# The weight panels' split moves from GpSimd to ScalarE and VectorE, in four slots

## What is computed

```
first block, per layer:
  x = x + 0.5 * swiglu(rmsnorm(x), w_ffn1_in, w_ffn1_out)          # D_FF = 2816
  h = rmsnorm(x);  proj = h @ w_in
  y_ret = (silu(rg) * rmsnorm(retention(rope(rq), rope(rk), rv))) @ w_o_ret    # 4 heads of 128
  y_fox = forgetting_attention(fq, fk, fv, log_sigmoid(ff + b)) @ w_o_fox      # 8 heads of 64
  x = x + (sigmoid(gate_r) * y_ret + sigmoid(gate_f) * y_fox) @ w_out
  x = x + 0.5 * swiglu(rmsnorm(x), w_ffn2_in, w_ffn2_out)
x = rmsnorm(x)
second block, per layer:
  h = rmsnorm(x) @ w_in_2, split into the inputs of four branches and a gate
  y = [window attention with sinks, gated convolution, latent attention, stick-breaking attention]
  x = x + rmsnorm((rmsnorm_per_group(y) * silu(gate)) @ w_out_2)
```

## Time and profile before

| | us |
|---|---|
| median of three runs | 3171.14 |
| the runs | 3172.47, 3171.14, 3154.9 |
| profiled execution, first to last instruction | 3161.7 |
| PE busy | 3000.1 (95%) |
| DVE busy | 1414.9 (45%) |
| ACT busy | 680.9 (22%) |
| POOL busy | 2047.7 (65%) |

### The profile page before, as it was taken

The page is one execution under the profiler, slowest core; times in us unless marked ns, Lnnn a source line. Parts: engine busy times, 40 slices in busy tenths (PEclk is TensorE's granted clock), DMA queues, the critical chain, the costliest instruction groups (busy, mean ns, idle before and its releaser), DMA issues.

```text
span 3161.7 us, 38115 instructions
## 1 busy us (share of the span) xinstructions
PE 3000.1 (95%) x13442; PEld 2394.4 (76%) x13442; DVE 1414.9 (45%) x1627; ACT 680.9 (22%) x1190; POOL 2047.7 (65%) x925
## 2 busy tenths in 40 slices
PE   7999988999999999999998899999998999989996
PEld 5888876778788887888877677778886877777775
DVE  6442234544744405443054534654415444554445
ACT  2221002122122201221002122222200223422253
POOL 5777765636777777877775535777776643365324
PEclk9999999999999999999999999999999999999998
DMA  3222222112222222222221211222222211122111
GB/s 127 93 93 93 93 100 71 66 47 74 93 88 97 93 93 81 94 96 95 93 104 67 71 49 60 93 93 93 93 93 86 74 54 42 46 75 73 47 34 54
DMA packets 69361, 251.59 MB, mean 80 GB/s; under 512 B 7696, under 2 KB 7824, under 8 KB 69008
## 3 DMA queue, kind: packets, MB, share of 16 engines
q1 hardware_dynamic: 68400, 246.46, 22.9%
q10 hardware_dynamic: 864, 3.79, 0.3%
HBM read 248.13 MB, written 2.10 MB: 79 GB/s over the span
## 4 chain that ended last, share of the span: by engine, by line
PE 82%; DVE 12%; issue 4%; ACT 1%; DVEq 0%; DMA 0%; ACTq 0%; SPq 0%
PE bank L459 22%; PE bank L460 22%; PE bank L461 22%; DVE xh L1377 2%; DVE ssq L1397 2%; PE bank L559 1%; PE bank L614 1%; PE bank L802 1%; PE bank L561 1%; PE bank L560 1%; PE bank L624 1%; PE bank L591 1%; PE bank L680 1%; DVE qr L1477 1%; PE bank L732 1%
## 5 line engine op out<-in xcount | busy, mean ns | idle before, releaser
L438 POOL TENSOR_TENSOR wh<-raw,one 128x1024 fp32r<-128x1024 f32 x460 | 885.2, 1924 | 1048.0 <-PE bank L461 964.3
L442 POOL TENSOR_TENSOR wl<-raw,wh 128x1024 fp32r<-128x1024 f32 x460 | 1162.3, 2527 | 36.1
L459 PE MATMUL bank<-xh,wh 128*128 128x512 f32 x2384 | 960.5, 403 | 23.9 <-DVE start_d L1945 10.5
L460 PE MATMUL bank<-xl,wh 128*128 128x512 f32 x2384 | 948.0, 398 | 0.0
L461 PE MATMUL bank<-xh,wl 128*128 128x512 f32 x2384 | 947.3, 397 | 0.0
L459 PEld LDWEIGHTS bank<-xh,wh 128*128 128x128 f32 x2384 | 452.3, 190 | 139.9 <-DVE xl L1379 23.3
L461 PEld LDWEIGHTS bank<-xh,wl 128*128 128x128 f32 x2384 | 451.5, 189 | 109.5
L460 PEld LDWEIGHTS bank<-xl,wh 128*128 128x128 f32 x2384 | 452.3, 190 | 106.3 <-issue 1.9
L460 PE MATMUL bank<-ul,wh 128*128 (+1 forms) x704 | 280.9, 399 | 0.0
L459 PE MATMUL bank<-uh,wh 128*128 (+1 forms) x704 | 277.4, 394 | 0.0
L461 PE MATMUL bank<-uh,wl 128*128 (+1 forms) x704 | 276.0, 392 | 0.0
(11 more groups left out here) (356 smaller groups left out, 3369.2 us busy)
## 6 DMA issues: line engine op xcount, KB each, us to landing
raw<-stream SPq DMA_DIRECT2D x460, 512.0 KB, 3.3
x<-x_t SPq DMA_DIRECT2D x4, 512.0 KB, 8.6
dec<-decay ACTq DMA_DIRECT2D x2, 1024.0 KB, 5.2
out<-x SPq DMA_DIRECT2D x8, 256.0 KB, 2.0
rp<-rope ACTq DMA_DIRECT2D x2, 512.0 KB, 6.4
cst<-const SPq DMA_DIRECT2D x1, 708.5 KB, 10.6
ffraw<-ff_w ACTq DMA_DIRECT2D x2, 316.0 KB, 7.4
posi<-pos SPq DMA_DIRECT2D x1, 256.0 KB, 11.2
```

Of the source, the lines that this page charges most:

```text
L438: pool.tensor_tensor(wh[:, slot, :], raw[:, n, :], one[:].to_broadcast([P, PANEL]), ALU.mult)\
L442: pool.tensor_tensor(wl[:, slot, :], raw[:, n, :], wh[:, slot, :].bitcast(F32), ALU.subtract).then_inc(split_lo, 1)
L459: pe.matmul(o, wh[:, s, c], rhs_h, start=first, stop=False)
L460: pe.matmul(o, wh[:, s, c], rhs_l, start=False, stop=False)
```

## The change

POOL does nothing any more. A panel's `wh` is made by `high` on ACT, a copy that rounds, and its `wl` by `low` on DVE, a subtraction. Both are placed by hand between the other steps of these engines, for the panel `LEAD = 3` behind the one that PE has reached there. `wh` and `wl` have four slots each instead of two, `raw` two instead of four, and `wl` is allocated before `wh`. `At` is a position in the stream as fours plus a rest, so that slot numbers stay known inside loops. The loops over the hybrid layers, the `rg` heads, the squares and the middle pairs of `forgetting` are written out; `ffn_in` on ACT goes two pairs at a time and the inner loop of `ffn_out` four panels at a time.

```diff
-RAW_SLOTS, SPLIT_SLOTS = 4, 2
+RAW_SLOTS, SLOTS = 2, 4
+LEAD = 3
+class At:
+    def __add__(self, panels):
+        return At(self.four, self.more + panels)
+    def fours(self, count):
+        return At(self.four + count, self.more)
+    def slot(self):
+        return self.more % SLOTS
+    def done(self, panels=1):
+        return self.four * SLOTS + (self.more + panels)
+    def raw(self):
+        return self.more % RAW_SLOTS
...
-        @block.gpsimd
-        def _(pool):
-            def split(n, g, first=False):
-                slot = n % SPLIT_SLOTS
-                pool.wait_ge(raw_in[n], 16 * (g + 1))
-                if not (first and n < SPLIT_SLOTS):
-                    pool.wait_ge(panel_done, g * RAW_SLOTS + (n + 1 - SPLIT_SLOTS))
-                pool.tensor_tensor(wh[:, slot, :], raw[:, n, :], one[:].to_broadcast([P, PANEL]), ALU.mult)\
-                    .then_inc(split_hi, 1)
-                pool.wait_ge(split_hi, g * RAW_SLOTS + (n + 1))
-                pool.tensor_tensor(wl[:, slot, :], raw[:, n, :], wh[:, slot, :].bitcast(F32),
-                                   ALU.subtract).then_inc(split_lo, 1)
...
@@ ACT @@
+            def high(at, first=False):
+                act.wait_ge(raw_in[at.raw], at.landed())
+                if not first:
+                    act.wait_ge(panel_done, at.done(1 - SLOTS))
+                act.activation(wh[:, at.slot, :], raw[:, at.raw, :], ACT.Copy).then_inc(split_hi, 1)
...
@@ DVE @@
+            def low(at):
+                dve.wait_ge(split_hi, at.done())
+                dve.tensor_tensor(wl[:, at.slot, :], raw[:, at.raw, :], wh[:, at.slot, :].bitcast(F32),
+                                  ALU.subtract).then_inc(split_lo, 1)
...
@@ ffn_in on ACT @@
+                def pair(j, at, first):
+                    if not first:
+                        high(at + LEAD)
                     act.wait_ge(*fin.at(it, "A"))
                     act.activation(sa[:], ta[:], ACT.Silu).then_inc(fin_act.sem, 1)
+                    high(at + 1 + LEAD)
                     act.wait_ge(*fin.at(it, "U"))
                     act.activation(uh[:, j, :], u32[:], ACT.Copy).then_inc(fin_act.sem, 1)
...
@@ ffn_in on DVE @@
                     scaled(ta[:], a[:], fin)
+                    if not first:
+                        low(at + LEAD)
                     scaled(tb[:], b[:], fin)
                     dve.tensor_tensor(u32[:], sa[:], tb[:], ALU.mult).then_inc(fin.sem, 1)
+                    low(at + 1 + LEAD)
                     dve.tensor_tensor(ul[:, j, :], u32[:], uh[:, j, :].bitcast(F32), ALU.subtract)\
...
@@ ffn_out on DVE, behind the steps of residual tile d @@
                     add_squares(n, d)
+                    for p in rest_done(d):
+                        low(idx + KT_MAJOR + p + LEAD)
...
@@ hybrid on DVE, behind the rotations of the latent queries @@
+                ahead(BT_UQ)
                 for i in range(2):
                     dve.scalar_tensor_tensor(out=dq[:, i, :], in0=bank[i][:], scalar=BDH ** -0.5, in1=rstd[:],
                                              op0=ALU.mult, op1=ALU.mult).then_inc(pj.sem, 1)
+                    ahead(BT_DQ + i)
...
@@ hybrid on ACT, ahead of the Silus of the gates @@
+                ahead(BT_GATE + KD - 2, 2)
                 for d in range(KD):
                     act.wait_ge(*gate_in.at(m * KD + d, "G"))
                     act.activation(gates[:, d, :], gates[:, d, :], ACT.Silu).then_inc(gate_s.sem, 1)
...
@@ start on DVE @@
                 prepare(0, d, 0)
+                if d == 0:
+                    low(At(0, 0))
             for d in range(KD):
                 add_squares(0, d)
+                if d in (4, 7):
+                    low(At(0, d // 3))
+            low(At(0, LEAD))
```

More of the change, by code:

```diff
@@ L671, in forgetting @@
                 pair(0, True, False)
[L672 removed]
+                for t2 in range(1, pairs - 1):
                     pair(t2, False, False)
@@ L1040, in _ @@
             chain_bc(FINAL, 7)
-            with pe.Fori(0, DEPTH) as m:
+            for m in range(DEPTH):
                 hybrid(m)
@@ L1135, in pair @@
                         fox_probs(it + 1, 0)
+                high(idx + LEAD)
+                high(idx + 1 + LEAD)
                 fox_probs(l * pairs, 0)
                 pair(0, True, False)
-                with act.Fori(1, pairs - 1) as t2:
+                for t2 in range(1, pairs - 1):
                     pair(t2, False, False)
@@ L1191, in hybrid, with ahead @@
                 n = FINAL + 1 + m
+                q0 = At(0, SECOND + m * LAYER2)
+                def ahead(tile, tiles=1):
+                    for i in range(tile, tile + tiles):
+                        if q0.more + i + LEAD < N_PANELS:
+                            high(q0 + i + LEAD)
+                ahead(BT_TM + (m == 0), 3 + (m > 0))
                 chain_std(n, 0, hyb_sq.at(m, "U"))
                 for i in range(2):
+                    ahead(BT_CQ + i)
                     act.wait_ge(*pj.at(m, f"Q{i}"))
                     act.activation(qsq[:, i, :], cq[:, i, :], ACT.Square).then_inc(lat_act.sem, 1)
+                ahead(BT_CKV)
                 act.wait_ge(*pj.at(m, "KV"))
                 act.activation(ksq[:], ckv[:], ACT.Square).then_inc(lat_act.sem, 1)
+                ahead(BT_AK)
                 act.wait_ge(*lat_pe.at(m, "COL"))
@@ L1321, in _ @@
             act.activation(start_a[:], eps[:], ACT.Copy).then_inc(rg_act.sem, 1)
-            squares(0)
+            high(At(0, 0), True)
+            squares(0, lambda d: d in (3, 7) and high(At(0, d // 4 + 1), True))
+            high(At(0, LEAD), True)
             act.wait_ge(const_in, 16)
@@ L1338, in _ @@
                 act.dma_start(ffraw[:], ff_w[l]).then_inc(tab_in, 16)
+                high(p0 + AT_RV + LEAD)
                 chain_std(l * 3 + 1, 0)
-                with act.Fori(0, RH) as h:
+                for p in range(1, KD):
+                    high(p0 + AT_RV + p + LEAD)
+                for h in range(RH):
+                    high(p0 + AT_RG + h + LEAD)
                     act.wait_ge(*rg.at(l * RH + h, "T"))
@@ L1366, in _ @@
             operands(0)
-            with act.Fori(0, DEPTH) as m:
+            for m in range(DEPTH):
                 hybrid(m)
@@ L1438, in ffn_in @@
                     for q in range(2):
-                        pair(i * 2 + q, bank[2 * q], bank[2 * q + 1], idx + i * 4 + 2 * q)
+                        pair(i * 2 + q, bank[2 * q], bank[2 * q + 1], (idx + 2 * q).fours(i))
             def ffn_out(f, n, idx):
+                with dve.Fori(0, KT_MAJOR // SLOTS) as i:
+                    for q in range(SLOTS):
+                        low((idx + q + LEAD).fours(i))
                 rest = KF - KT_MAJOR
@@ L1691, in hybrid, with ahead @@
             def hybrid(m):
-                q0 = SECOND + m * LAYER2
+                q0 = At(0, SECOND + m * LAYER2)
                 n = FINAL + 1 + m
-                norm_chain(n, 1)
-                dve.wait_ge(panel_done, q0 + BT_TM + KD // 2)
+                def ahead(tile, tiles=1):
+                    for i in range(tile, tile + tiles):
+                        if q0.more + i + LEAD < N_PANELS:
+                            low(q0 + i + LEAD)
+                ahead(BT_TM + (m == 0), 2 + (m > 0))
+                norm_chain(n, 1, lambda: ahead(BT_TM + 3))
+                dve.wait_ge(panel_done, (q0 + BT_TM).done(KD // 2))
                 for t in range(TT):
@@ L2020, in _ @@
                     operand_lo(0, d - 1)
-            with dve.Fori(0, DEPTH) as m:
+            for m in range(DEPTH):
                 hybrid(m)
```

357 lines of the change are left out of this document (209 added, 148 removed).

## The result

| | kernel before | changed kernel |
|---|---|---|
| median (lowest to highest), us | 3166.4 (3154.9 to 3172.5), 4 runs | 3045.9 (3044.0 to 3048.0), 4 runs |
| ratio of the runs, 95% interval | | 0.9619 [0.9591, 0.9648] |
| span of the profiled execution | 3161.7 | 3044.6 (its time 3046.4) |

The change is worth 120 us by the medians and 117.1 us between the two profiled spans.

What follows compares the result with a forecast made beforehand. TensorE was taken as the bound, busy 3000.1 of 3161.7 us, its waits due to GpSimd slowing DVE. Stage gains less give-backs sum to 84.4 us: from a median of 3171 to 3087, range 3062 to 3126 (8 of 10).

Steps and rivals of the forecast that it cites:

- The cause: DVE steps on two SBUF tiles wait out GpSimd's step in progress; the same add takes 0.69 or 2.77 us.
- the costs of the new steps: Per panel, ACT's copy `wh` takes 1.06 us and DVE's subtraction `wl` 1.23 us.
- the steady state at no cost: Within the feed-forward the new split keeps up with PE, with about 9 us of slack; cost nothing.
- the seams of the feed-forward: Gains: ends into the mixer 20.7 us, into the second block 6.4, start of layer 2 6.2.
- the wait at the third latent panel: Hybrid layers, ahead of `dq`: PE idles about 2.0 us for a `wl` in place of 6.8.
- No rival: Alternatives: late seams 3125 (0.22); GpSimd not the cause 3196 (0.03); raw-slot loop 3225 (0.03); more gain 3067 (0.10).
- the fourth's 3067: No PE wait in the gating or before panel 1, clock up all through: 20 us less; chance 0.10.
- matmuls at 0.233 us: Matmul pace stays at 0.233 us; another pace would prove the prediction wrong.
- head 0 of the retention: Decay chain shrinks 5.4 us, two `low` add 2.5: 2.9 gained, 3.8 of the 6.64 wait and low clock stay.
- The start: Kernel start: 2.5 us gained, despite a first `low` delaying PE 1.2 and a wait of some 5 for panel 1.
- `dq`: Both hybrid layers: PE's 6.78 us waits for rotations shrink by 4.8 each, 9.5 us together.
- The hybrid layers' rest: Shorter `spl` steps gain 7.5 us and the gating gives back 2.6 in both layers: 4.9.

Runs made afterwards that it cites:

- e1: Changed kernel with an unused 128x1 tensor where the removed `one` stood, so tiles behind it start 32 bytes further on; 3056.6 us.
- e9: Changed kernel with the `low` inside each rotation moved behind the product with the swapped halves; 3051.2 us.
- e2: Kernel before, with `uh`, merged heads and head outputs shifted to 0 modulo 256 and ACT's loop over the retention-gate Silus written out; 3146.6 us.
- e14: Kernel before, GpSimd's split untouched, with all big TensorE operands at the same place modulo 256 (distance 0); 3143.4 us.
- e10: Changed kernel with a second 128x1024 subtraction, read by nobody, behind each `low` on DVE but the first four; 3089.9 us.
- e3: Changed kernel with unused 128-byte tensors ahead of `x` and `raw`, so `xh` and `xl` start at 0 modulo 256 instead of 128; 3024.4 us.
- e12: Changed kernel with `wl` and `wh` 192 bytes further on, at 128 modulo 256 instead of 192, all else in place; 3022.5 us.
- e7: Changed kernel with `xh`, `xl`, `ygh` and `ygl` at 0 modulo 256 and panel 1's split made earlier at the start; 3020.8 us.
- e5: Changed kernel with `wl` back on GpSimd as its subtraction, `wh` staying on ACT and no `low` on DVE; 3077.4 us.

## Why the prediction was right in kind and short by 33 us

**What held.** The cause (a DVE step of two SBUF tiles waits GpSimd's step out), the costs of the new steps (1.06 and 1.23 forecast, 1.05 and 1.22 measured), the steady state at no cost, and the seams of the feed-forward: 20.7 forecast and 21.3 measured, 6.4 and 6.7, 6.2 and 5.1. GpSimd is empty, `ssq` is not waited for at the mixer, the wait at the third latent panel is there. No rival came true: the time lies below even the fourth's 3067, but PE still waits for panel 1 (4.2 us) and in the gating (2.0).

**The failed step: "matmuls at 0.233 us" for all of them.** The text named another pace as what would prove it wrong, and so it was: 2880 matmuls at 0.2289 instead of 0.2333 us, 12.7 us by count, 10.7 in e1. The forecast had put this term at nothing. The diff shows that tiles move (`one` goes, slots change), and the trace of before shows two paces at clock 1.00, 0.233 in `ffn_in` and 0.230 in the token-major stage. I read both and took the difference to be one of the kind of matmul.

**The step mis-sized most: head 0 of the retention**, "five steps of two SBUF tiles shrink by the mean 1.09", "and two `low` add 2.5: 2.9 gained, some 3.8 of 6.64 stay". It gained 6.7 of wait and 2.1 of clock in each layer, 8.8 for 2.9. DVE before, then after:

```profile
493.50 1.94 DVE L1986 SCALAR_TENSOR_TENSOR fq<-fq 72x512 f32<-72x512 f32 x1 [6.58 <-ACT fq L1348]
495.48 3.30 DVE L1989 TENSOR_TENSOR_SCAN cum<-cst,fq 72x512 f32<-72x512 f32 x1
...
501.74 1.86 DVE L1475 TENSOR_TENSOR diag<-tq,rp 128x512 f32<-128x512 f32 x1
```
```profile
471.20 0.69 DVE L2114 SCALAR_TENSOR_TENSOR fq<-fq 72x512 f32<-72x512 f32 x1 [4.08 <-ACT fq L1431]
471.92 1.22 DVE L2117 TENSOR_TENSOR_SCAN cum<-cst,fq 72x512 f32<-72x512 f32 x1
...
476.10 0.69 DVE L1567 TENSOR_TENSOR diag<-tq,rp 128x512 f32<-128x512 f32 x1
476.71 1.22 DVE L1454 TENSOR_TENSOR wl<-raw,wh 128x1024 fp32r<-128x1024 f32 x1
```

Three errors, all one way. The mean was taken where single rows stood: the scan alone shrank by 2.08, the five steps by 7.6. The `low` was priced in full at 1.23, and cost some 0.4 (e9). And the chain began 1.4 us earlier, counted at the same place of PE's work, because a table load of 1.28 us on ACT ahead of it went. Of ACT's 153 table loads 104 went: in the loops before, each round loaded its table anew (88 loads in `ffn_in`, 8 for the retention gates), and with the rounds, or the first ones of a loop, written out 4 and 2 are left. The chain adds up to the 6.7: 1.4 of start, 3.3 of the first step and the scan, nothing in Q's rotation, 2.0 in K's. With no wait the clock stayed up as well.

**Smaller ones.** The start: 2.5 forecast, 7.5 measured, of it 0.9 from the earlier `x` and 3.7 because the eight sums of squares and the 24 matmuls behind them no longer run at half clock (0.9 and 5.7 us, 1.9 and 8.4 before). `dq`: 11.9 for 9.5, with the forecast 2 us wait at 1.73. The hybrid layers' rest, 0.8 for 4.9: the waits for `spl` went as counted, but a new wait of 1.28 us for `lsg` came in each layer. Behind it the clock stayed up in the first layer; in the last, two groups of eight products take 4.63 us each where they took 2.42, half clock, 4.4 us together. The rows, after and before:

```profile
2905.38 2.84 PE L822 MATMUL bank<-vtm,lsg 128*128 128x64 f32 x20 [1.28 <-ACT lsg L1349]
2908.15 4.63 PE L797 MATMUL bank<-dq,dk 64*128 64x512 f32 x8
```
```profile
3031.39 2.42 PE L788 MATMUL bank<-dq,dk 64*128 64x512 f32 x8
```

## What to carry to other kernels

Read single rows where a chain decides, and ask of every added step what the engine would be waiting for at that moment; a mean over 88 rows and a full price gave a third of the truth. What GpSimd costs DVE depends on which of its steps a chain meets, so the loss jumps with small shifts (e2), and it can eat a gain made elsewhere (e14). A total that comes out as expected says little while its terms have not been read (e10). When a change moves tiles, compare the matmuls' pace in full windows at clock 1.00, and put moving and stationary operands at the same place modulo 256: in the changed kernel it was worth 46 us more.

## What the runs showed of the hardware

The pace of a 128x512 fp32r matmul with a weight load for each depends on how the two operands lie to each other: 0.227, 0.229 or 0.233 us (e1, e3, e12, with the one exception in e7). The Trainium skill (TensorE: Matmul & The Clock Gate, "Wait — 56ns, not 53.3ns?") has 215.7 ns for back-to-back matmuls of 512 columns; the best here is 5% above it. GpSimd and DVE lengthen each other's steps (`u` 0.69 to 1.88 us, GpSimd's subtraction 2.53 to 2.85), ACT's don't change (1.051 and 1.056). Of the clock: behind waits for `kr` of 1.2 to 1.9 us the eight score matmuls took 2.42 us each time (e5, e9), behind 2.18 once 2.42 and once 3.65 (e10), behind 2.94 both 4.63 and 2.42. The length of the wait alone doesn't settle it: behind the one of 1.28 us for `lsg` in the last hybrid layer the products took 4.63.
